# Feed-forward activation turned by VectorE block transposes and SBUF-to-SBUF DMAs instead of TensorE transposes

## The chip, the core and the metric

The kernel runs on one core of one Trainium2 chip. The metric is the device time of one execution in microseconds (us), and lower is better. Engines are named as the profile names them: PE is TensorE (PEld its weight loads), DVE is VectorE, ACT is ScalarE, POOL is GpSimd, SP is SyncE, which here only issues DMAs. A name with a q (ACTq, SPq) is the engine's instruction sequencer.

## What is computed

Two decoder layers over 256 tokens of width 2048, all in float32. Each layer has a mixer and then a SwiGLU feed-forward part; the change lies in the latter alone:

```python
h = rms_norm(x, ffn_norm[l])
gate, up = jnp.split(h @ w_gate_up[l], 2, axis=-1)      # w_gate_up: 2048 x 11264
x = x + ((jax.nn.silu(gate) * up) @ w_down[l]).astype(x.dtype)   # w_down: 5632 x 2048
```

## The kernel before

**Matmuls.** Every large weight is split into a high part `w_hi` and a remainder `w_lo`, and so is every activation, and each product is three matmuls: high by high, high by low, low by high (lines 1475 to 1477). The stationary operand is a 128x128 piece of the turned activation, the moving one 512 columns of the weight. A *slot* is 1 MB of weights, four rows of 128 by 512 columns; it is handled in two *halves*, and PE does 12 matmuls for each half.

**The weight pipeline.** SP loads slot j into one of four places of `raw` (line 338), once VectorE has finished the slot that lay there. ACT rounds a half to `w_hi` (`half_hi`, line 451, after waits for the load and for `half_used`), DVE subtracts it from `raw` to make `w_lo` (`half_lo`, line 890), and PE multiplies. `w_hi` and `w_lo` are rings of four halves, so ACT and DVE write at most four halves ahead of PE: the half (2,0), meaning slot j = 2 and its first half, can be written only when PE has done the half (0,0). In the code `half_used` counts the halves that PE has done.

**The feed-forward part.** The 5632 inner columns are 11 chunks of 512. Each layer does them in two parts, of 6 and of 5 chunk pairs (`PAIRS`). A *pair* is one chunk of gate, slots j = 0 to 3, and the same chunk of up, slots j = 4 to 7. The first pair of a part is written out; the others are a hardware loop on every engine. After its pairs a part multiplies its activation with `w_down`: four output chunks c, each of as many slots as the part has pairs (the *down* phase). There are 22 pairs in all, 18 of them turned inside a loop, 4 of them in a down phase.

**The activation between gate/up and down.** ACT makes `silu` of the gate from PSUM (lines 828, 829) ahead of slot 6. When up is complete, DVE multiplies: two operations write `act_row`, 256 tokens by 512 columns, tokens on partitions (`act_rows`, lines 1402 and 1403). This stands in DVE's program ahead of slot 2 of the next pair, or of slot 2 of the down phase. The down matmul wants columns on partitions, so `act_row` is turned: PE does eight 128x128 transposes into PSUM banks 4 and 5 (`turn`, line 2004), after slot 3 of the next pair, or ahead of slot 3 of the down phase. ACT then copies them to `act_hi` (`turned_hi`, line 840), ahead of slot 6, or after slot 3 in the down phase. DVE writes `act_lo` (`turned_lo`, line 1410). PE waits for `act_lo` ahead of the last slot of output chunk 0.

Each engine runs its own instructions in the order in which the code writes them, and semaphores tie them together. There is no scheduler.

Of the kernel before, what the change touches and what calls it, by code (L numbers as in the profile page):

```python
# [27 lines left out]
F32 = mybir.dt.float32  # L28
# [7 lines left out]
P = 128  # L36
D = 2048
SEQ = 256
TT = SEQ // P
DEPTH = 2  # L40
KT = D // P
CH = 512
# [70 lines left out]
def build(nc, stream, x_in, positions, params, consts, lora, gains, rows, out):  # L113
    with ExitStack() as ctx:
# [49 lines left out]

        gain_row = gain[0:2 * DEPTH * KT, 0:P]
        rstd = small[:, 220:222]
        p_rw = at(RING_END, RW_F, TT, P)
        p_mla = at(RING_END + 3584, TT, 832)
        p_hg = at(RING_END + 5248, TT, 2048)
# [271 lines left out]
        def _(act):  # L441
# [66 lines left out]
            for l in range(DEPTH):  # L508
# [306 lines left out]
                for part, pairs in enumerate(PAIRS):  # L815
                    fresh = part == 0
                    makes_norm = part == len(PAIRS) - 1 and l < DEPTH - 1

                    def pair(i, first):
                        gi, si = i * 2 + g4f, i * 2 + s4f  # L820
                        for j in range(8):
                            if j == 6:

                                act.wait_ge(half_used, chunk_ends(si, 4))
                                if not (first and pair0 == 0):
                                    act.wait_ge(S("act_row_ready"), i + pair0)
                                act.wait_ge(S("rstd_ready"), norm_of_ffn + 1)
                                nc.scalar.activation(silu[:, 0, :], psum[:, 0, :], ACT.Silu, scale=rstd[:, 0:1])
                                nc.scalar.activation(silu[:, 1, :], psum[:, 1, :], ACT.Silu, scale=rstd[:, 1:2]).then_inc(
                                    acc_free[0], 1)  # L830
                                if not first:
                                    turned_hi(i - 1, pair0)
                            split_hi(gi, si, j)
                            if first and fresh:
                                norm_tail(norm_of_ffn, j)

                    def turned_hi(i, p0):
                        act.wait_ge(S("act_turned"), i + (p0 + 1))
                        dst = act_hi[:, bass.ds(i * 4, 4), :] if not isinstance(i, int) else act_hi[:, 4 * i:4 * i + 4, :]
                        nc.scalar.activation(dst, bank(4, 2).rearrange("p (k t) -> p k t", k=4),  # L840
                                             ACT.Copy).then_inc(S("act_hi_ready"), 1)

                    pair(0, True)
                    with act.Fori(1, pairs) as i:
                        pair(i, False)
                    g4f, s4f = g4f + 2 * pairs, s4f + 2 * pairs
                    for j in range(4 * pairs):
                        split_hi(g4f, s4f, j)
                        if j == 3:
                            turned_hi(pairs - 1, pair0)  # L850
                        if makes_norm and j > pairs and j % pairs == 3:
                            x_hi(2 * l + 2, j // pairs - 1)
                            x_squares(2 * l + 2, j // pairs - 1)
                    g4f, s4f = g4f + pairs, s4f + pairs
                    pair0 += pairs
# [3 lines left out]
        def _(dve):  # L859
# [108 lines left out]
            for l in range(DEPTH):  # L968
# [426 lines left out]
                for n, pairs in enumerate(PAIRS):  # L1395
                    def act_rows(i, si, p0):

                        dve.wait_ge(half_used, chunk_ends(si, 8))
                        dve.wait_ge(acc_free[0], i + (gate_base + 2))
                        if not isinstance(i, int) or i + p0 > 0:  # L1400
                            dve.wait_ge(S("act_turned"), i + p0)
                        stt(act_row[:, 0, :], psum[:, 2, :], rstd[:, 0:1], silu[:, 0, :], MUL, MUL)
                        stt(act_row[:, 1, :], psum[:, 3, :], rstd[:, 1:2], silu[:, 1, :], MUL, MUL).then_inc(acc_free[1], 1)
                        dve.wait_ge(acc_free[1], i + (gate_base + 2))
                        dve.sem_inc(S("act_row_ready"), 1)

                    def turned_lo(i, p0):
                        dve.wait_ge(S("act_hi_ready"), i + (p0 + 1))
                        k = bass.ds(i * 4, 4) if not isinstance(i, int) else slice(4 * i, 4 * i + 4)
                        tt(act_lo[:, k, :], bank(4, 2).rearrange("p (k t) -> p k t", k=4), act_hi[:, k, :].bitcast(F32),  # L1410
                           SUB).then_inc(S("act_lo_ready"), 1)

                    gate_base = odd0 + sum(PAIRS[:n]) + 4 * n // 2
# [42 lines left out]
        def _(pe):  # L1456
# [81 lines left out]
            for l in range(DEPTH):  # L1538
# [456 lines left out]
                for part, pairs in enumerate(PAIRS):  # L1995
                    makes_norm = part == len(PAIRS) - 1 and l < DEPTH - 1

                    def turn(i, p0):
                        pe.wait_ge(S("act_row_ready"), i + (p0 + 1))
                        if not isinstance(i, int) or i + p0 > 0:  # L2000
                            pe.wait_ge(S("act_lo_ready"), i + p0)
                        for k in range(4):
                            for t in range(TT):
                                last = tr(bank(4, 2)[:, k * SEQ + t * P:k * SEQ + (t + 1) * P],  # L2004
                                          act_row[:, t, k * P:(k + 1) * P], ident)
                        last.then_inc(S("act_turned"), 1)

                    def pair(i, first):
                        si = i * 2 + s4f
                        for u in range(2):  # L2010
                            pe.wait_ge(acc_free[u], i + (acc + 1))
                            if part == 0 and first and u == 0:
                                for j in range(4):
                                    first_slot(2 * l + 1, si, j, 0)
                            else:
                                slots(si, range(4 * u, 4 * u + 4), 0, KT, 2 * u, hT_hi, hT_lo)
                            if u == 0 and not first:
                                turn(i - 1, pair0)

                    pair(0, True)  # L2020
                    with pe.Fori(1, pairs) as i:
# [2 lines left out]
                    for c in range(4):  # L2024
                        pe.wait_ge(acc_free[c % 2], acc + c // 2 + 1)
                        for j in range(pairs):
                            if c == 0 and j == 3:
                                turn(pairs - 1, pair0)
                            if c == 0 and j == pairs - 1:
                                pe.wait_ge(S("act_lo_ready"), pair0 + pairs)  # L2030
                            if l == DEPTH - 1 and part == len(PAIRS) - 1 and c == 3 and j == pairs - 1:
                                last_slot(s4f, pairs * c + j, 4 * j, 4 * pairs, 2 * (c % 2), act_hi, act_lo)
                                continue
                            slots(s4f, [pairs * c + j], 4 * j, 4 * pairs, 2 * (c % 2), act_hi, act_lo)
                            if makes_norm and c and j == 1:
                                x_turn(2 * l + 2, c - 1)
# [99 lines left out]
```

## Time and profile before

| | us |
|---|---|
| median of 3 runs | 2353.47 |
| range of the runs | 2352.15 to 2355.67 |
| span of the profiled execution | 2351.5 |
| PE busy in it | 2324.1 |
| DVE busy | 1331.0 |
| ACT busy | 1103.5 |

The span goes from the first to the last instruction. Busy times are sums over one engine's instructions. The columns in a view of the timeline are start, duration, engine, line and operation, output and input, and in brackets how long the engine sat idle before it and what ended that. A DMA's own row is the time in which the issuing sequencer was taken; its landing is counted from the issue.

### The profile page before, as it was taken

The page shows a single profiled execution, that of the slowest core. Times are in us where ns is not written, and L with a number is a line of the kernel's source. Part 1 is how long each engine was busy: PE and PEld are TensorE (multiplying, and loading weights), DVE is VectorE, ACT ScalarE, POOL GpSimd, SP SyncE. Part 2 cuts the span into 40 slices and gives each one's busy share as a digit, 9 for nine tenths or more (in the row PEclk, how much of TensorE's full clock was granted, in tenths as well). Part 3 has the DMA queues.
Part 4 walks back from the last instruction along what each step waited for, and adds up shares of the span by engine and source line. Part 5 has one row for each costly group of instructions (what it writes and reads, how often), then busy time and mean ns, then how long its engine had stood idle before and what let it go on. Part 6 is the DMA issues. An engine that isn't in the chain of part 4 may idle for free.

```text
span 2351.5 us, 33396 instructions
## 1 busy us (share of the span) xinstructions
PE 2324.1 (99%) x13481; PEld 1924.8 (82%) x13481; DVE 1331.0 (57%) x1420; ACT 1103.5 (47%) x1362; POOL 55.1 (2%) x58
## 2 busy tenths in 40 slices
PE   8999999999999999999999999999999999999999
PEld 7888688888888888888888886888888888888887
DVE  5686676545445445445557857765454454454454
ACT  6554745544443344444445547454444433444433
POOL 0000110000000000000000002100000000000000
PEclk9999999999999999999999999999999999999999
DMA  7453305555555555554554532044555555555554
GB/s 299 166 184 130 122 21 178 181 195 194 182 195 182 194 196 193 184 194 181 193 184 152 194 115 102 29 171 180 196 189 186 193 184 194 197 191 185 192 184 141
DMA packets 59519, 407.04 MB, mean 173 GB/s; under 512 B 6608, under 2 KB 6704, under 8 KB 13200
## 3 DMA queue, kind: packets, MB, share of 16 engines
q1 hardware_dynamic: 58720, 401.66, 47.9%
q0 software_dynamic: 688, 3.78, 0.5%
q8 instruction: 84, 1.38, 0.2%
q14 instruction: 27, 0.22, 0.0%
HBM read 403.32 MB, written 2.10 MB: 172 GB/s over the span
## 4 chain that ended last, share of the span: by engine, by line
PE 93%; DVE 5%; issue 1%; ACT 0%; DMA 0%; DVEq 0%; SPq 0%; ACTq 0%
PE psum L1475 28%; PE psum L1477 28%; PE psum L1476 28%; PE psum L1669 2%; PE psum L1917 1%; PE psum L2004 1%; PE psum L1764 1%; PE psum L1570 1%; PE psum L1509 1%; DVE arena L1211 1%; DVE arena L1284 0%; DVE arena L1292 0%; DVE small L1194 0%; DVE arena L1188 0%; DVE arena L1178 0%
## 5 line engine op out<-in xcount | busy, mean ns | idle before, releaser
L890 DVE TENSOR_TENSOR w_lo<-raw,w_hi 128x1024 fp32r<-128x1024 f32 (+2 forms) x752 | 901.3, 1205 | 843.9 <-ACT w_hi L451 836.8
L451 ACT ACTIVATE w_hi<-raw 128x1024 fp32r<-128x1024 f32 (+2 forms) x752 | 782.0, 1044 | 1071.8 <-PE psum L1477 1070.2
L1475 PE MATMUL psum<-w_hi,hT_hi 128*128 128x512 f32 (+2 forms) x2128 | 821.6, 386 | 3.1 <-DVE w_lo L890 3.1
L1477 PE MATMUL psum<-w_hi,hT_lo 128*128 128x512 f32 (+2 forms) x2128 | 816.4, 384 | 0.0
L1476 PE MATMUL psum<-w_lo,hT_hi 128*128 128x512 f32 (+2 forms) x2128 | 816.3, 384 | 0.0
L1475 PEld LDWEIGHTS psum<-w_hi,hT_hi 128*128 128x128 f32 x2128 | 399.7, 188 | 81.8 <-DVE w_lo L890 2.4
L1477 PEld LDWEIGHTS psum<-w_hi,hT_lo 128*128 128x128 f32 x2128 | 399.6, 188 | 78.5
L1476 PEld LDWEIGHTS psum<-w_lo,hT_hi 128*128 128x128 f32 x2128 | 399.8, 188 | 76.4
L1475 PE MATMUL psum<-w_hi,act_hi 128*128 128x512 f32 x872 | 340.4, 390 | 0.0
L1477 PE MATMUL psum<-w_hi,act_lo 128*128 128x512 f32 x872 | 339.4, 389 | 0.0
L1476 PE MATMUL psum<-w_lo,act_hi 128*128 128x512 f32 x872 | 339.3, 389 | 0.0
L1477 PEld LDWEIGHTS psum<-w_hi,act_lo 128*128 128x128 f32 x872 | 163.7, 188 | 33.9
L1476 PEld LDWEIGHTS psum<-w_lo,act_hi 128*128 128x128 f32 x872 | 163.7, 188 | 33.7
L1475 PEld LDWEIGHTS psum<-w_hi,act_hi 128*128 128x128 f32 x872 | 163.7, 188 | 33.7
L1669 PE MATMUL psum<-raw,arena 128*128 128x384 f32 (+1 forms) x192 | 72.0, 525 | 0.4
L1669 PEld LDWEIGHTS psum<-raw,arena 128*128 128x128 f32 x192 | 35.3, 190 | 30.9 <-issue 11.8
L1410 DVE TENSOR_TENSOR act_lo<-psum,act_hi 128x1024 f32 (+1 forms) x22 | 26.9, 1224 | 38.6 <-ACT act_hi L840 38.6
L1764 PEld LDWEIGHTS psum<-arena 64*64 64x64 f32 x1024 | 33.3, 142 | 4.0 <-DVE arena L1269 2.2
L1764 PE MATMUL psum<-arena 64*64 64x64 f32 x1024 | 35.3, 227 | 0.6 <-DVE arena L1269 0.6
L902 DVE SCALAR_TENSOR_TENSOR hT_lo<-psum,gain_col,hT_hi 128x256 fp32r<-128x256 f32 x64 | 26.5, 476 | 14.0 <-ACT hT_hi L473 14.0
L840 ACT ACTIVATE act_hi<-psum 128x1024 f32 (+1 forms) x22 | 22.6, 1027 | 20.8 <-PE psum L2004 20.8
L923 DVE TENSOR_TENSOR x<-x,psum 128x1024 f32<-128x1024 f32 x23 | 27.9, 1213 | 4.9 <-PE psum L1477 4.9
(319 smaller groups left out, 1194.7 us busy)
## 6 DMA issues: line engine op xcount, KB each, us to landing
raw<-stream_dram SPq DMA_DIRECT2D x360, 1024.0 KB, 4.8
raw<-stream_dram SPq DMA_DIRECT2D x16, 512.0 KB, 3.7
raw<-stream_dram SPq DMA_DIRECT2D x8, 768.0 KB, 4.3
raw<-stream_dram SPq DMA_DIRECT2D x8, 640.0 KB, 3.8
x<-x_in_dram SPq DMA_DIRECT2D x4, 512.0 KB, 9.2
lor<-lora_dram POOLq DMA_DIRECT2D x2, 832.0 KB, 10.3
con<-consts_dram POOLq DMA_DIRECT2D x1, 1648.0 KB, 11.4
out_dram<-x SPq DMA_DIRECT2D x3, 512.0 KB, 7.3
```

The source lines that it names most:

```text
L451: nc.scalar.activation(w_hi[:, q % HALF_RING, 0:2 * w], raw[:, j % 4, hf * 2 * w:(hf + 1) * 2 * w], ACT.Copy).then_inc(hi_done, 1)
L890: tt(w_lo[:, q % HALF_RING, 0:2 * w], raw[:, j % 4, hf * 2 * w:(hf + 1) * 2 * w], w_hi[:, q % HALF_RING, 0:2 * w].bitcast(F32), SUB).then_ ...
L902: last = stt(hT_lo[:, 4 * c + k, :], bank(x_turn_bank(n, c), 2)[:, k * SEQ:(k + 1) * SEQ], gain_col[:, n * KT + 4 * c + k:n * KT + 4 * c + ...
L923: vs(tt(xs, xs, psum[:, b0:b0 + 2, :], ADD), "x_added", n_added)
L1211: u(ts(z, z, small[:, 64 + off + h:65 + off + h], None, MUL))
L1410: tt(act_lo[:, k, :], bank(4, 2).rearrange("p (k t) -> p k t", k=4), act_hi[:, k, :].bitcast(F32), SUB).then_inc(S("act_lo_ready"), 1)
L1475: mm(o, a_hi, w_hi[:, r, cols], start=(k == 0), stop=False)
L1476: mm(o, a_hi, w_lo[:, r, cols], start=False, stop=False)
L1477: last = mm(o, a_lo, w_hi[:, r, cols], start=False, stop=(k == n_k - 1))
L1509: last = tr(bank(x_turn_bank(n, c), 2)[:, k * SEQ + t * P:k * SEQ + (t + 1) * P], x[:, t, c * CH + k * P:c * CH + (k + 1) * P], ident)
L1669: last = mm(psum[:, UP_BANK[c] + t, 0:w], src[:, k, t * P:(t + 1) * P], raw[:, c % 4, k * w:(k + 1) * w], start=(k == 0), stop=(k == nk - 1))
L1764: last = mm(bank(b0, 2)[hp, m * w:(m + 1) * w], left(hp, n), right(hp, n), start=True, stop=True)
```

## The change

PE no longer turns the activation. `act_row` is written in another layout, one `STREAM_TRANSPOSE` on DVE turns every 32x32 block of it into `act_blocks`, and 16 DMAs from SBUF to SBUF, 32 partitions by 256 elements (32 KB) each, put the blocks on their partitions in `act_moved`. ACT issues these 16 after its slot 2. `turned_hi` and `turned_lo` then read `act_moved` instead of PSUM. The two buffers lie in `gain`, which the feed-forward part doesn't use otherwise.

```diff
+        act_blocks = gain[:, 0:2 * CH]
+        act_moved = gain[:, 2 * CH:4 * CH]
+        n_moves = (P // 32) ** 2
...
                             split_hi(gi, si, j)
+                            if j == 2 and not first:
+                                move_blocks(i - 1, pair0)
...
+                    def move_blocks(i, p0):
+
+                        act.wait_ge(S("act_blocks_turned"), i + (p0 + 1))
+                        if not isinstance(i, int) or i + p0 > 0:
+                            act.wait_ge(S("act_lo_ready"), i + p0)
+                        for q in range(P // 32):
+                            for b in range(P // 32):
+                                act.dma_start(act_moved[32 * q:32 * q + 32, 256 * b:256 * b + 256],
+                                              act_blocks[32 * b:32 * b + 32, 256 * q:256 * q + 256]).then_inc(
+                                                  S("act_moved"), 16)
+
                     def turned_hi(i, p0):
-                        act.wait_ge(S("act_turned"), i + (p0 + 1))
-                        dst = act_hi[:, bass.ds(i * 4, 4), :] if not isinstance(i, int) else act_hi[:, 4 * i:4 * i + 4, :]
-                        nc.scalar.activation(dst, bank(4, 2).rearrange("p (k t) -> p k t", k=4),
+                        act.wait_ge(S("act_moved"), i * (16 * n_moves) + 16 * n_moves * (p0 + 1))
+                        k = bass.ds(i * 4, 4) if not isinstance(i, int) else slice(4 * i, 4 * i + 4)
+                        nc.scalar.activation(act_hi[:, k, :].rearrange("p k (t b e) -> p (k t) b e", t=TT, e=32),
+                                             act_moved.rearrange("p (b n e) -> p n b e", n=8, e=32),
                                              ACT.Copy).then_inc(S("act_hi_ready"), 1)
...
                     for j in range(4 * pairs):
                         split_hi(g4f, s4f, j)
+                        if j == 2:
+                            move_blocks(pairs - 1, pair0)
                         if j == 3:
                             turned_hi(pairs - 1, pair0)
...
-                        stt(act_row[:, 0, :], psum[:, 2, :], rstd[:, 0:1], silu[:, 0, :], MUL, MUL)
-                        stt(act_row[:, 1, :], psum[:, 3, :], rstd[:, 1:2], silu[:, 1, :], MUL, MUL).then_inc(acc_free[1], 1)
+                        for t in range(TT):
+                            last = stt(act_row.rearrange("p a b -> p (a b)").rearrange(
+                                "p (n t r) -> p t n r", n=16, t=TT)[:, t],
+                                psum[:, 2 + t, :].rearrange("p (n r) -> p n r", n=16), rstd[:, t:t + 1],
+                                silu[:, t, :].rearrange("p (n r) -> p n r", n=16), MUL, MUL)
+                        last.then_inc(acc_free[1], 1)
                         dve.wait_ge(acc_free[1], i + (gate_base + 2))
                         dve.sem_inc(S("act_row_ready"), 1)
+                        nc.vector.transpose(act_blocks.rearrange("p (q k n) -> p k q n", q=4, k=4),
+                                            act_row.rearrange("p a b -> p (a b)").rearrange(
+                                                "p (k q n) -> p k q n", k=4, q=4)).then_inc(
+                            S("act_blocks_turned"), 1)
+                        dve.wait_ge(S("act_blocks_turned"), i + (p0 + 1))
...
-                    def turn(i, p0):
-                        pe.wait_ge(S("act_row_ready"), i + (p0 + 1))
-                        if not isinstance(i, int) or i + p0 > 0:
-                            pe.wait_ge(S("act_lo_ready"), i + p0)
-                        for k in range(4):
-                            for t in range(TT):
-                                last = tr(bank(4, 2)[:, k * SEQ + t * P:k * SEQ + (t + 1) * P],
-                                          act_row[:, t, k * P:(k + 1) * P], ident)
-                        last.then_inc(S("act_turned"), 1)
...
-                            if u == 0 and not first:
-                                turn(i - 1, pair0)
...
-                            if c == 0 and j == 3:
-                                turn(pairs - 1, pair0)
```

Line numbers in the listings of the changed program are its own; in them L456 is the old line 451, L911 the old 890, L1504 to L1506 the old 1475 to 1477, and `gain` is where `act_blocks` and `act_moved` lie.

On ACT, inside the loop over pairs, from slot 2 to slot 3. Before:

```order
L450 REGISTER_ALU [waits raw_in2]
L451 ACTIVATE w_hi<-raw 128x1024 [waits half_used]
L450 REGISTER_ALU [waits raw_in2]
L451 ACTIVATE w_hi<-raw 128x1024 [waits half_used]
L450 REGISTER_ALU [waits raw_in3]
L451 ACTIVATE w_hi<-raw 128x1024 [waits half_used]
```

And in the changed program:

```order
L455 REGISTER_ALU [waits raw_in2]
L456 ACTIVATE w_hi<-raw 128x1024 [waits half_used]
L455 REGISTER_ALU [waits raw_in2]
L456 ACTIVATE w_hi<-raw 128x1024 [waits half_used]
L848 REGISTER_ALU [waits act_blocks_turned]
L851 DMA gain<-gain 32x256 [waits act_lo_ready]
L851 DMA gain<-gain 32x256 x15
L455 REGISTER_ALU [waits raw_in3]
L456 ACTIVATE w_hi<-raw 128x1024 [waits half_used]
```

Sixteen DMA issues and a wait for DVE now stand between the half (2,1) and the half (3,0).

On PE, inside the same loop, between slot 3 and slot 4, the last matmul of gate and the first of up. Before:

```order
L1477 MATMUL psum<-w_hi,hT_lo 128x512
L2001 REGISTER_ALU [waits act_row_ready]
L2004 MATMUL psum<-con,act_row 128x128 [waits act_lo_ready]
L2004 MATMUL psum<-con,act_row 128x128 x7
L1467 REGISTER_ALU [waits acc_odd_free]
L1475 MATMUL psum<-w_hi,hT_hi 128x512 [waits w_lo_written]
```

And in the changed program:

```order
L1506 MATMUL psum<-w_hi,hT_lo 128x512
L1496 REGISTER_ALU [waits acc_odd_free]
L1504 MATMUL psum<-w_hi,hT_hi 128x512 [waits w_lo_written]
```

The eight transposes and the two waits ahead of them are gone, and nothing took their place on PE.

On DVE, in the changed program's loop, where the activation is multiplied, just ahead of `w_lo` of the half (2,0):

```order
L1420 REGISTER_ALU [waits half_used]
L1422 SCALAR_TENSOR_TENSOR act_row<-psum,small,silu 128x16x32 [waits acc_even_free]
L1422 SCALAR_TENSOR_TENSOR act_row<-psum,small,silu 128x16x32
L1429 STREAM_TRANSPOSE gain<-act_row 128x4x4x64 [waits acc_odd_free]
L910 REGISTER_ALU [waits act_blocks_turned]
L911 TENSOR_TENSOR w_lo<-raw,w_hi 128x1024 [waits w_hi_written]
```

The block transpose is new; it waits for the two products, and the next half's `w_lo` waits for it.

## Rows read from the trace of the kernel before

**Rows 1.** The page: its head, and the busy time of each engine.

```profile
span 2351.5 us, 33396 instructions
PE 2324.1 (99%) x13481; PEld 1924.8 (82%) x13481; DVE 1331.0 (57%) x1420; ACT 1103.5 (47%) x1362; POOL 55.1 (2%) x58
```

**Rows 2.** Busy time by stretch: stretch, engines, granted clock, DMA share, GB/s.

```profile
423.00:904.00 481.00, 481.00 (x2156) 398.90 (x2154) 239.86 (x211) 204.65 (x213) 0.00 (x0) 1.00 0.54 190
```

**Rows 3.** The page's costliest groups: count, busy and mean ns, idle time before.

```profile
L890 DVE TENSOR_TENSOR w_lo<-raw,w_hi 128x1024 fp32r<-128x1024 f32 (+2 forms) x752 | 901.3, 1205 | 843.9 <-ACT w_hi L451 836.8
L451 ACT ACTIVATE w_hi<-raw 128x1024 fp32r<-128x1024 f32 (+2 forms) x752 | 782.0, 1044 | 1071.8 <-PE psum L1477 1070.2
```

**Rows 4.** Timeline of PE around one turn inside the loop.

```profile
514.36 0.39 PE L1477 MATMUL psum<-w_hi,hT_lo 128*128 128x512 f32 x1
514.59 1.03 PE L2004 MATMUL psum<-con,act_row 128*128 128x128 f32 x8
515.38 0.48 PE L1475 MATMUL psum<-w_hi,hT_hi 128*128 128x512 f32 x1
515.70 0.40 PE L1476 MATMUL psum<-w_lo,hT_hi 128*128 128x512 f32 x1
515.93 0.39 PE L1477 MATMUL psum<-w_hi,hT_lo 128*128 128x512 f32 x1
```

**Rows 5.** All instructions of line 2004: count, ns min/median/max, first and last start.

```profile
L2004 PE MATMUL psum<-con,act_row x176: 270/272/276, 514.6 to 2255.4; 128*128 128x128 f32 x176
```

**Rows 6.** Timeline of DVE over one pair of the loop.

```profile
495.26 0.74 DVE L1402 SCALAR_TENSOR_TENSOR act_row<-psum,small,silu 128x512 f32<-128x512 f32 x1
495.92 0.74 DVE L1403 SCALAR_TENSOR_TENSOR act_row<-psum,small,silu 128x512 f32<-128x512 f32 x1
496.89 1.23 DVE L890 TENSOR_TENSOR w_lo<-raw,w_hi 128x1024 fp32r<-128x1024 f32 x1 [0.22 <-ACT w_hi L451]
...
539.67 0.74 DVE L1402 SCALAR_TENSOR_TENSOR act_row<-psum,small,silu 128x512 f32<-128x512 f32 x1
```

**Rows 7.** Timeline of ACT there: halves (2,0), (2,1) and (3,0).

```profile
495.75 1.06 ACT L451 ACTIVATE w_hi<-raw 128x1024 fp32r<-128x1024 f32 x1 [1.66 <-PE psum L1477]
498.46 1.06 ACT L451 ACTIVATE w_hi<-raw 128x1024 fp32r<-128x1024 f32 x1 [1.66 <-PE psum L1477]
501.19 1.06 ACT L451 ACTIVATE w_hi<-raw 128x1024 fp32r<-128x1024 f32 x1 [1.66 <-PE psum L1477]
```

**Rows 8.** All instructions of line 1284, DVE's block transposes in the mixer.

```profile
L1284 DVE STREAM_TRANSPOSE arena<-arena x18: 711/711/1245, 289.6 to 1499.0; 128x512 f32<-128x512 f32 x16, 128x1024 f32<-128x1024 f32 x2
```

**Rows 9.** Register operations of ACT's sequencer at line 450, from 519 to 524 us.

```profile
L450 ACTq ALU_OP  x2: 35/35/35, 521.1 to 523.8; - x2
```

**Rows 10.** All issues of line 338, in the feed-forward part, and their landing.

```profile
L338 SPq DMA_DIRECT2D raw<-stream_dram x264: 332/333/352, 423.1 to 2318.2; - x132
...
DMA to landing us min/median/max: 4.6/4.8/6.5
```

**Rows 11.** Timeline of SP's first DMA issues, back to back.

```profile
0.75 0.58 SPq L315 DMA_DIRECT2D gain<-gains_dram  x1
1.38 0.57 SPq L313 DMA_DIRECT2D x<-x_in_dram  x1
...
5.51 22.52 SPq L332 DMA_DIRECT2D raw<-stream_dram  x5
```

**Rows 12.** Timeline of POOL: its DMA issues back to back, first and last of six.

```profile
20.85 0.54 POOL L374 DMA_DIRECT2D con<-consts_dram  x1 [18.87 <-DMA raw<-stream_dram]
...
23.50 0.54 POOL L383 DMA_DIRECT2D lor<-lora_dram  x1
```

**Rows 13.** Landing of line 315's one DMA, 32 KB.

```profile
DMA to landing us min/median/max: 2.0/2.0/2.0
```

**Rows 14.** Timeline of ACT in a down phase: halves (2,0), (3,1), `act_hi`, (4,0).

```profile
717.92 1.06 ACT L451 ACTIVATE w_hi<-raw 128x1024 fp32r<-128x1024 f32 x1 [1.66 <-PE psum L1477]
...
726.09 1.06 ACT L451 ACTIVATE w_hi<-raw 128x1024 fp32r<-128x1024 f32 x1 [1.66 <-PE psum L1477]
732.35 1.03 ACT L840 ACTIVATE act_hi<-psum 128x1024 fp32r<-128x1024 f32 x1 [5.20 <-PE psum L2004]
733.27 2.96 ACT L451 ACTIVATE w_hi<-raw 128x1024 fp32r<-128x1024 f32 x3
```

More of the change, by code:

```diff
@@ L1399, in act_rows @@
                         dve.wait_ge(acc_free[0], i + (gate_base + 2))
-                        if not isinstance(i, int) or i + p0 > 0:
-                            dve.wait_ge(S("act_turned"), i + p0)
-                        stt(act_row[:, 0, :], psum[:, 2, :], rstd[:, 0:1], silu[:, 0, :], MUL, MUL)
-                        stt(act_row[:, 1, :], psum[:, 3, :], rstd[:, 1:2], silu[:, 1, :], MUL, MUL).then_inc(acc_free[1], 1)
+                        for t in range(TT):
[4 more added lines that the diff above has]
+                        last.then_inc(acc_free[1], 1)
                         dve.wait_ge(acc_free[1], i + (gate_base + 2))
                         dve.sem_inc(S("act_row_ready"), 1)
+                        nc.vector.transpose(act_blocks.rearrange("p (q k n) -> p k q n", q=4, k=4),
[3 more added lines that the diff above has]
+                        dve.wait_ge(S("act_blocks_turned"), i + (p0 + 1))
                     def turned_lo(i, p0):
@@ L1409, in turned_lo @@
                         k = bass.ds(i * 4, 4) if not isinstance(i, int) else slice(4 * i, 4 * i + 4)
-                        tt(act_lo[:, k, :], bank(4, 2).rearrange("p (k t) -> p k t", k=4), act_hi[:, k, :].bitcast(F32),
+                        hi, lo = (z[:, k, :].rearrange("p k (t b e) -> p (k t) b e", t=TT, e=32) for z in (act_hi, act_lo))
+                        tt(lo, act_moved.rearrange("p (b n e) -> p n b e", n=8, e=32), hi.bitcast(F32),
                            SUB).then_inc(S("act_lo_ready"), 1)
@@ L1996, in _ @@
                     makes_norm = part == len(PAIRS) - 1 and l < DEPTH - 1
-                    def turn(i, p0):
-                        pe.wait_ge(S("act_row_ready"), i + (p0 + 1))
-                        if not isinstance(i, int) or i + p0 > 0:
-                            pe.wait_ge(S("act_lo_ready"), i + p0)
-                        for k in range(4):
-                            for t in range(TT):
-                                last = tr(bank(4, 2)[:, k * SEQ + t * P:k * SEQ + (t + 1) * P],
-                                          act_row[:, t, k * P:(k + 1) * P], ident)
-                        last.then_inc(S("act_turned"), 1)
                     def pair(i, first):
```

## The prediction, made before the change was run

> **What bounds the kernel now.** I read the page first, then the busy time by stretch, then the timeline of one pair. The page has PE busy for 2324.1 of 2351.5 us and the next engine, DVE, for 1331.0 [rows 1]. In a stretch wholly inside the feed-forward part PE is busy for 481.00 of 481.00 us, at a granted clock of 1.00, its 2.4 GHz level, while DVE and ACT are busy for half or less of it [rows 2]. The costliest groups say who waits for whom: ACT's `w_hi` was idle 1071.8 us, nearly all until PE had used a half, and DVE's `w_lo` 843.9 us until ACT had written one [rows 3]. So in this part PE sets the pace and the other two stand ready four halves ahead. Whatever leaves PE shortens the kernel by its full time, as long as no weight half comes late. Whatever is added to ACT or DVE is free until it has eaten that lead.
>
> **What is removed: 22 turns on PE.** In the timeline, neighbouring matmuls start 0.227 us apart. Without the turn the matmul after the one at 514.36 would start at 514.59, and the two behind it at 514.81 and 515.04. They start at 515.38, 515.70 and 515.93 [rows 4], and from there on the old step is back. So one turn takes 515.93 - 515.04 = 0.89 us from PE, less than the 1.03 us of its row, since its ends overlap with the neighbours. The same comes out another way: from one pair's product to the next is 539.67 - 495.26 = 44.41 us [rows 6], and 16 halves of 2.72 us (501.19 - 495.75 over two, [rows 7]) are 43.52. There are 176 transposes, eight to a turn, so 22 turns [rows 5], and 22 x 0.89 = 19.5 us.
>
> Rows 4 and 5 put one 128x128 transpose at 0.11 us of PE's time. The Trainium skill (VectorE: DVE Perf Modes, The three transpose paths) gives a bf16 one on TensorE as 390 ns; an estimate by that page would make the removal worth 22 x 8 x 0.39 = 69 us. The measured gaps decide against that. The same page's Rules for kernel authors advise TensorE for a 128x128 transpose if PSUM will do as its destination, which speaks against this change.
>
> **What is added on DVE.** The two products keep their size and count, so they stay at 0.74 us each [rows 6]; their output is in runs of 32 elements, and I take no extra for that. The block transpose of 128x1024 took 1245 ns in the mixer, and 711 ns for half of it [rows 8]. The new one has four dimensions; I take 1.25 us, and even twice that would be hidden: `w_lo` of the half (2,0) now starts at about 496.9 + 1.25 = 498.1 instead of 496.89, and ends at 499.4. I put PE's first matmul of this pair at 514.59 - 8 x 2.72 = 492.83, so it needs (2,0) at 492.83 + 4 x 2.72 = 503.7. Nothing is late.
>
> **What is added on ACT: 16 DMA issues, and this decides.** They stand between the halves (2,1) and (3,0). Queued behind them are (3,0) on ACT, `w_lo` of (3,0) on DVE, and PE. The time they may take, in the clock of [rows 7]:
> - Start. The blocks are turned at about 498.2. ACT's sequencer gets past the half (2,1) when that starts, at 498.46. Register operations ran at 521.1 and 523.8 [rows 9], one for each half's start and not all at once, so the sequencer does not pass a waiting instruction, but it need not wait for a running one to end. So the issues start at about 498.55; if a DMA must wait for the running operation to end, at 498.46 + 1.06 = 499.52.
> - End. PE needs (3,0) at 492.83 + 6 x 2.72 = 509.15. From `w_hi`'s start to `w_lo`'s end is (496.89 + 1.23) - 495.75 = 2.37 us [rows 6, 7]. So ACT must be free by 506.78.
>
> This leaves 8.23 us, or 0.51 us for each issue, with the earlier start, and 7.26 us, or 0.45 us, with the later. No row shows an issue on ACT. The nearest, from below: SP's issues of 1 MB in this same part took 0.333 us each, alone [rows 10]; with a gap of 0.05 us between two (1.38 - 0.75 - 0.58, [rows 11]) that is 0.38 us, and 16 are 6.1 us. From above: SP's first eight issues, back to back, came every (5.51 - 0.75) / 8 = 0.595 us [rows 11], and 16 are 9.5 us. In between lies POOL, which generates its own descriptors: (23.50 - 20.85) / 5 = 0.53 us [rows 12], 8.5 us. I take 0.38 us. The 264 issues of [rows 10] are in the same stage and within 20 ns of each other, while the slow ones of [rows 11] stand at the cold start and move far larger pieces, of mixed tensors. Then ACT is free at 504.6 (505.6 with the later start), 2.1 (1.2) us ahead of need, and catches up at once, because a half takes it 1.06 us and PE 2.72. That it can catch up is on record: in a down phase ACT stood still until 732.35 for the turned activation and then wrote three halves in 2.96 us [rows 14], with PE never idle in that stretch [rows 2]. The cost at 0.38 us is nothing. Beyond 0.51 (0.45) us each further 0.1 us costs 1.6 us in each of the 22 turns.
>
> **The transfers.** 16 DMAs of 32 KB are 0.5 MB in a pair whose weights are 8 MB. A 32 KB load landed 2.0 us after issue [rows 13], so the last block lands at about 506.6; by the slowest weight load, 6.5 us [rows 10], at 511. Inside the loop ACT asks for them ahead of slot 6, whose half (6,0) stands 6 x 2.72 us behind (3,0)'s 501.19, at about 517, which is late enough for both. In a down phase it asks after (3,1). There the old wait lasted until 732.35, which is 14.43 us after (2,0) at 717.92 [rows 14], or 510.2 in the clock used above. Landing at 506.6 is 3.6 us earlier than the old turn; landing at 511 is 0.9 us later, four times in the kernel, at most 4 us. For the weight loads the DMA share is 0.54 [rows 2] and they land in 4.8 us; a place in `raw` is freed some 16.7 us ahead of its use (7 halves of 2.72 less the 2.37 us of chain), so they stay hidden.
>
> The Trainium skill (DMA: Bandwidth & Descriptors, Measured) says that transfers under 64 KB are dominated by their descriptors. By it these copies move slowly; since their landing has slack, the sum stays as it is.
>
> `turned_hi` and `turned_lo` read SBUF instead of PSUM. ACT and DVE already do this shape from SBUF in 1.06 and 1.23 us [rows 6, 7], so I count nothing.
>
> **The sum.** Span 2351.5 - 19.5 = 2332.0 us. The median of the runs is 2.0 us above this span, so **2334.0 us** against 2353.5, or 0.83% less.
>
> **Rival 1: ACT's issues become PE's wait, and the kernel is slower.** Place: the half (3,0) of each of 22 turns. It costs more than it brings when 16 issues exceed 8.23 + 0.89 = 9.12 us, 0.57 us each (with the later start 8.15 us, 0.51 us). At the 0.595 us of [rows 11] the wait is 9.52 - 8.23 = 1.29 us, the net +0.40 a turn, 2362; with the later start 2.26 us, +1.37 a turn, 2384. For it: those eight rows are the only back-to-back ones on a sequencer of this kind, and sixteen at once is what the change does. Against it: [rows 10]. An issue of 1 us would give some 2500 and I leave it beyond the range. Chance 0.27. It is also how the rule for TensorE, cited above, would come true.
>
> **Rival 2: issues of about 0.53 us eat most of the gain.** At POOL's pace [rows 12] the wait is 0.25 us, and the result 2353.5 - 22 x 0.64 = 2339; with the later start the wait is 1.22 us and the result 2361. So one price ends on either side. What ends within 0.2% of before needs a wait of 0.68 to 1.10 us a turn, a narrow band. Chance 0.09.
>
> **Rival 3: the turned activation comes late in the down phases.** By the bounds above at most about 4 us, so 2338, still faster. Chance 0.04.
>
> **Rival 4: the change doesn't do what it says.** The transposes do leave PE, but another wait could stand in the same place: the accumulator banks of up, which DVE frees with the second product at 496.66, 18 us before PE wants them. That leaves no room for it. Chance 0.01.
>
> **How the numbers follow.** The forecast, no new wait on PE, has 0.59. Rival 2 has 0.09, of which 0.03 lie on the faster side and 0.06 within 0.2%. With rival 3 (0.04, faster) and rival 4 (0.01, within) faster by over 0.2% has 0.66, within 0.2% 0.07, and slower by over 0.2% 0.27, rival 1's. 0.2%, 4.7 us, is about what a measurement of this kernel can tell from no change. The range runs from 2331, since nothing but the turns leaves PE and 3 us covers the reading of the 0.89, to 2375, which takes in rival 2 and the lower half of rival 1; the upper half stays out with about 0.13, and what lies under 2331 with 0.03. The likeliest case's own range is 2331 to 2340.
>
> **What would show each step right or wrong.** The turns: line 2004 gone and PE's starts 0.227 us apart from gate to up. The cover: PE's row of waits for `w_lo` stays at a few us in all; if rival 1 holds, it shows PE idle 22 times ahead of the half (3,0), released by `w_lo`. The price: the duration and the spacing of ACTq's DMA issues, 0.38 us forecast, 0.51 where it begins to cost, and whether the first starts beside the half (2,1) or behind it. DVE: a block transpose of about 1.25 us, 22 times. The landing: ACT's wait for the moved blocks, none in the loop, and in the down phases shorter than the 5.2 us that the old one took [rows 14]. The forecast fails if an issue on ACT takes over 0.5 us, if the weight loads land so late that ACT waits for `raw`, or if the granted clock falls below 1.00.

## Result and profile after

| | before | changed |
|---|---|---|
| median of the runs, us | 2354.57 | 2419.98 |
| range of the runs, us | 2352.15 to 2355.80 | 2416.43 to 2424.21 |
| span of the profiled execution, us | 2351.5 | 2414.9 |
| mean granted PE clock | 0.999 | 0.986 |

The ratio is 1.0279, with a 95% interval of 1.0264 to 1.0294: 2.8% slower, where 0.8% faster was forecast. The time lies beyond the range's end at 2375.

The page of the changed kernel, its head, engines, the chain that ended last, and the groups that answer to [rows 1, 3]:

```profile
span 2414.9 us, 33409 instructions
PE 2339.1 (97%) x13305; PEld 1925.2 (80%) x13305; DVE 1351.7 (56%) x1442; ACT 1095.2 (45%) x1362; POOL 55.0 (2%) x58
...
PE 81%; ACTq 9%; DVE 6%; ACT 1%; issue 1%; DMA 0%; SPq 0%; DVEq 0%
...
L456 ACT ACTIVATE w_hi<-raw 128x1024 fp32r<-128x1024 f32 (+2 forms) x752 | 775.7, 1043 | 1166.4 <-PE psum L1506 983.8
L1504 PE MATMUL psum<-w_hi,hT_hi 128*128 128x512 f32 (+2 forms) x2128 | 831.8, 391 | 41.4 <-DVE w_lo L911 41.4
...
L1504 PE MATMUL psum<-w_hi,act_hi 128*128 128x512 f32 x872 | 342.8, 393 | 10.8 <-DVE w_lo L911 10.8
```

The transposes are gone: 13305 matmuls instead of 13481, 176 fewer. But PE now stood idle 52.2 us (41.4 + 10.8) for `w_lo`, and ACT's sequencer, which had no share in the chain before, holds 9% of it. In the feed-forward part there are 22 waits, one ahead of each half (3,0). All three links of one such wait stand in the timelines of ACT, DVE and PE. ACT, from the half (2,0) of the second loop pair on:

```profile
543.42 1.07 ACT L456 ACTIVATE w_hi<-raw 128x1024 fp32r<-128x1024 f32 x1 [1.66 <-PE psum L1506]
546.14 1.06 ACT L456 ACTIVATE w_hi<-raw 128x1024 fp32r<-128x1024 f32 x1 [1.65 <-PE psum L1506]
546.22 10.29 ACTq L851 DMA_DIRECT2D gain<-gain  x16
556.63 3.90 ACT L456 ACTIVATE w_hi<-raw 128x1024 fp32r<-128x1024 f32 x4 [9.43 <-issue]
```

DVE over the same pair:

```profile
542.93 1.40 DVE L1422 SCALAR_TENSOR_TENSOR act_row<-psum,small,silu 128x512 f32<-128x512 f32 x2
544.49 1.25 DVE L1429 STREAM_TRANSPOSE gain<-act_row 128x1024 f32<-128x1024 f32 x1
545.86 1.23 DVE L911 TENSOR_TENSOR w_lo<-raw,w_hi 128x1024 fp32r<-128x1024 f32 x1
547.24 1.23 DVE L911 TENSOR_TENSOR w_lo<-raw,w_hi 128x1024 fp32r<-128x1024 f32 x1 [0.15 <-ACT w_hi L456]
557.72 4.63 DVE L911 TENSOR_TENSOR w_lo<-raw,w_hi 128x1024 fp32r<-128x1024 f32 x4 [9.26 <-ACT w_hi L456]
```

PE, at the half (3,0):

```profile
556.37 0.39 PE L1505 MATMUL psum<-w_lo,hT_hi 128*128 128x512 f32 x1
556.59 0.39 PE L1506 MATMUL psum<-w_hi,hT_lo 128*128 128x512 f32 x1
559.00 0.70 PE L1504 MATMUL psum<-w_hi,hT_hi 128*128 128x512 f32 x1 [2.02 <-DVE w_lo L911]
559.50 0.63 PE L1505 MATMUL psum<-w_lo,hT_hi 128*128 128x512 f32 x1
559.92 0.63 PE L1506 MATMUL psum<-w_hi,hT_lo 128*128 128x512 f32 x1
...
562.06 0.62 PE L1505 MATMUL psum<-w_lo,hT_hi 128*128 128x512 f32 x1
562.48 0.43 PE L1506 MATMUL psum<-w_hi,hT_lo 128*128 128x512 f32 x1
562.75 0.39 PE L1504 MATMUL psum<-w_hi,hT_hi 128*128 128x512 f32 x1
562.98 0.40 PE L1505 MATMUL psum<-w_lo,hT_hi 128*128 128x512 f32 x1
```

Sixteen issues keep ACT's sequencer for 10.3 us, `w_hi` of (3,0) starts at 556.63, its `w_lo` at 557.72, and PE, which was ready at about 556.8, starts at 559.00: 559.00 - 556.59 - 0.227 = 2.18 us late. Then something that the prediction had no price for: the next matmuls start 0.43 us apart instead of 0.227. The busy time by stretch (columns as in [rows 2]: PE, PEld, DVE, ACT, POOL, then the granted clock, DMA share and GB/s):

```profile
555.00:559.00 4.00, 1.98 (x10) 1.32 (x8) 1.28 (x2) 2.37 (x3) 0.00 (x0) 1.00 0.13 33
559.00:563.00 4.00, 4.00 (x11) 3.14 (x12) 3.35 (x3) 1.52 (x2) 0.00 (x0) 0.57 0.40 117
563.00:567.00 4.00, 4.00 (x19) 3.31 (x18) 1.23 (x1) 1.68 (x2) 0.00 (x0) 1.00 1.00 406
```

After 2 us of idleness the granted clock was 0.57 over 4 us, mostly the 1.2 GHz level, and then 1.00 again, the 2.4 GHz level. From 559.00 to 562.98 PE takes ten steps in 3.98 us where 2.27 were due, 1.71 us lost.

**The sum for this pair**: -0.89 (turn) + 2.18 (wait) + 1.71 (clock) = +3.0 us. For the whole kernel: 22 x -0.89 = -19.5; idle for `w_lo` 52.2 less the 3.1 of before [PE's row for line 1475 on the page of before], plus 0.16 us for each of 22 waits that the idle figure leaves out (2.18 against 2.02), +52.6; and behind 17 of the 22 waits PE's matmuls step at 0.43 us for a while, 17 x 1.71 = +29. Together +62; the spans differ by 63.4. (Added up one by one in the trace, the 17 come to 31 us: fifteen lost 1.5 to 1.8 us, two lost 2.6 and 3.0.)

The pair shown stands for most, but not for all. In 18 of the 22 turns the sixteen issues took 10.2 to 10.4 us and PE stood idle 1.9 to 2.2 us. In the first turn and in the last, a down phase's, of each layer they took 11.2 to 12.0 us, because single issues among them read up to 1.88 us, and PE stood idle 3.0 to 3.8 us. Why those issues are long is not shown.

### The profile page after: what moved, and what is told of

The parts are those of the page before. It is cut to its first block, busy times and chain, and to the rows that moved or that the text cites. A ratio compares the mean times of both kernels' runs of the same rounds, so it can differ in the third digit from the quotient of the medians.

```text
span 2414.9 us, 33409 instructions
## 1 busy us (share of the span) xinstructions
PE 2339.1 (97%) x13305; PEld 1925.2 (80%) x13305; DVE 1351.7 (56%) x1442; ACT 1095.2 (45%) x1362; POOL 55.0 (2%) x58
## 4 chain that ended last, share of the span: by engine, by line
PE 81%; ACTq 9%; DVE 6%; ACT 1%; issue 1%; DMA 0%; SPq 0%; DVEq 0%
PE psum L1504 25%; PE psum L1505 25%; PE psum L1506 25%; ACTq L851 9%; PE psum L1698 2%; DVE w_lo L911 1%; PE psum L1946 1%; ACT w_hi L456 1%; PE psum L1793 1%; PE psum L1599 1%; PE psum L1538 1%; DVE arena L1232 1%; DVE arena L1305 0%; DVE arena L1313 0%; DMA x<-x_in_dram 0%
## 5 line engine op out<-in xcount | busy, mean ns | idle before, releaser
L911 DVE TENSOR_TENSOR w_lo<-raw,w_hi 128x1024 fp32r<-128x1024 f32 (+2 forms) x752 | 896.2, 1204 | 905.8 <-ACT w_hi L456 895.5
L456 ACT ACTIVATE w_hi<-raw 128x1024 fp32r<-128x1024 f32 (+2 forms) x752 | 775.7, 1043 | 1166.4 <-PE psum L1506 983.8
L1504 PE MATMUL psum<-w_hi,hT_hi 128*128 128x512 f32 (+2 forms) x2128 | 831.8, 391 | 41.4 <-DVE w_lo L911 41.4
L1505 PE MATMUL psum<-w_lo,hT_hi 128*128 128x512 f32 (+2 forms) x2128 | 825.8, 388 | 0.0
L1506 PE MATMUL psum<-w_hi,hT_lo 128*128 128x512 f32 (+2 forms) x2128 | 825.4, 388 | 0.0
L1504 PEld LDWEIGHTS psum<-w_hi,hT_hi 128*128 128x128 f32 x2128 | 405.4, 190 | 129.8 <-DVE w_lo L911 48.6
L1506 PEld LDWEIGHTS psum<-w_hi,hT_lo 128*128 128x128 f32 x2128 | 405.3, 190 | 80.8
L1505 PEld LDWEIGHTS psum<-w_lo,hT_hi 128*128 128x128 f32 x2128 | 405.4, 191 | 78.7
L1504 PE MATMUL psum<-w_hi,act_hi 128*128 128x512 f32 x872 | 342.8, 393 | 10.8 <-DVE w_lo L911 10.8
L1506 PE MATMUL psum<-w_hi,act_lo 128*128 128x512 f32 x872 | 341.3, 391 | 0.0
L1504 PEld LDWEIGHTS psum<-w_hi,act_hi 128*128 128x128 f32 x872 | 165.0, 189 | 46.7 <-DVE w_lo L911 12.5
L1506 PEld LDWEIGHTS psum<-w_hi,act_lo 128*128 128x128 f32 x872 | 164.9, 189 | 34.6
L1439 DVE TENSOR_TENSOR act_lo<-gain,act_hi 128x1024 f32 (+1 forms) x22 | 26.9, 1224 | 18.4 <-ACT act_hi L858 18.4
L1422 DVE SCALAR_TENSOR_TENSOR act_row<-psum,small,silu 128x512 f32<-128x512 f32 x44 | 30.9, 743 | 0.0
## 6 DMA issues: line engine op xcount, KB each, us to landing
lor<-lora_dram POOLq DMA_DIRECT2D x2, 832.0 KB, 10.8
```

What stands on the lines that cost most here:

```text
L456: nc.scalar.activation(w_hi[:, q % HALF_RING, 0:2 * w], raw[:, j % 4, hf * 2 * w:(hf + 1) * 2 * w], ACT.Copy).then_inc(hi_done, 1)
L911: tt(w_lo[:, q % HALF_RING, 0:2 * w], raw[:, j % 4, hf * 2 * w:(hf + 1) * 2 * w], w_hi[:, q % HALF_RING, 0:2 * w].bitcast(F32), SUB).then_ ...
L1422: last = stt(act_row.rearrange("p a b -> p (a b)").rearrange("p (n t r) -> p t n r", n=16, t=TT)[:, t], psum[:, 2 + t, :].rearrange("p (n ...
L1439: tt(lo, act_moved.rearrange("p (b n e) -> p n b e", n=8, e=32), hi.bitcast(F32), SUB).then_inc(S("act_lo_ready"), 1)
L1504: mm(o, a_hi, w_hi[:, r, cols], start=(k == 0), stop=False)
L1505: mm(o, a_hi, w_lo[:, r, cols], start=False, stop=False)
```

## Experiments

**Theory A**: the issues hold ACT's sequencer longer than its lead over PE, PE waits for that, and the clock falls because PE waits. **Rival B**: DVE's longer block or the new reads from SBUF hold the pipeline. **Rival C**: the copies' traffic does. **Rival D**: the clock falls for another reason. Each experiment was timed beside the kernel before anew: it took 2352.1 us beside the first four, 2352.6 beside the next four, and 2353.6 in one run beside the last four. And one question inside theory A: why does an issue cost 0.61 us when SP's loads cost 0.333 [rows 10]?

### The change without its copies

```diff
-                        for q in range(P // 32):
-                            for b in range(P // 32):
-                                act.dma_start(act_moved[...], act_blocks[...]).then_inc(S("act_moved"), 16)
...
-                                             act_moved.rearrange("p (b n e) -> p n b e", n=8, e=32),
+                                             act_blocks.rearrange("p (b n e) -> p n b e", n=8, e=32),
```

> The changed kernel without its 16 copies: act_hi is read from the unmoved blocks, so the activation that goes into the down product is not the reference's. Everything else of the change stays: the new layout of act_row, DVE's block transpose, act_hi and act_lo from SBUF. Theory A (the time in which ACT issues the copies is what PE waits for, and the clock falls after the wait): no wait at all, the full gain of the turns, 2334 us. Rival B (DVE's longer block, or the new reads from SBUF, hold the pipeline): PE still waits for w_lo, 2380 us or more.

Measured: 2332.1 us, ratio 0.9913 (0.9897 to 0.9930). PE never waits in the feed-forward part; what it is idle for `w_lo` elsewhere, 3.1 us, is the 3.1 us of the kernel before. So DVE's block transpose, the new layouts and the reads from SBUF cost nothing: rival B falls. This is also the whole gain that the removal of the turns can give, 2352.1 - 2332.1 = 20.0 us against the forecast 19.5.

### The kernel before, with the issues added

```diff
                             split_hi(gi, si, j)
+                            if j == 2 and not first:
+                                move_blocks(i - 1, pair0)
...
                     def turned_hi(i, p0):
+                        act.wait_ge(S("act_moved"), i * (16 * n_moves) + 16 * n_moves * (p0 + 1))
                         act.wait_ge(S("act_turned"), i + (p0 + 1))
```

> The kernel before, with its TensorE turns, plus the 16 copies a pair on ACT at the changed kernel's place; nothing reads what they copy, ACT only waits for them ahead of act_hi. Theory A: ACT is taken for 10.3 us, PE waits 2.0 us idle in each of 22 pairs and the clock falls after most of them, so 2354 + 22 x (2.2 + 1.3) + the rest = 2430 to 2440 us. Rival B: without the block transpose the wait disappears, 2354 us.

Measured: 2421.6 us, ratio 1.0300 (1.0282 to 1.0317). The sixteen copies alone, with TensorE's turns kept and DVE untouched, bring the loss. It is a little under what was expected: only 10 of the 22 waits were followed by matmuls at 0.43 us, against 17 in the changed kernel, and the four waits in the down phases lasted 1.1 us only. What decides whether a wait of 2 us costs the clock isn't shown.

### The same issues, spread over ACT's halves

```diff
+LOOP_MOVES = {5: (0, 4), 6: (4, 7), 7: (7, 10), 8: (10, 12), 9: (12, 14), 10: (14, 16)}
+DOWN_MOVES = {5: (0, 6), 6: (6, 11), 7: (11, 16)}
...
+                            for hf in range(2):
+                                half_hi(gi, si, j, hf)
+                                if not first and 2 * j + hf in LOOP_MOVES:
+                                    move_blocks(i - 1, pair0, *LOOP_MOVES[2 * j + hf])
```

> The changed kernel with the same 16 issues on ACT, but 4, 3, 3, 2, 2, 2 of them behind six successive halves of the loop, from (2,1) on, and 6, 5, 5 behind three halves in a down phase, where act_hi and act_lo then come behind the first half of slot 4. Theory A: no half is late by more than the lead, 2334 us, or up to 2345 if the down phases lose some. Rival C (the copies' traffic, or the sequencer time in total, is what costs): as the changed kernel, about 2420 us. It also shows the price of an issue that follows a pause.

Measured: 2336.8 us, ratio 0.9930 (0.9913 to 0.9946). Same 352 copies, same engine, and PE waits for no `w_lo` in the feed-forward part: rival C falls, and ACT's total sequencer time is no problem, only its length in one piece. Two new waits stand in its down phases:

```profile
PE psum L1510 <- DVE act_lo L1444: 3.9, 2, 2.4
```

There `act_hi` comes later than in the changed kernel, behind the first half of slot 4, and it waited for the copies to land. That wait, with one fall of the clock behind it (1.5 us), is about what this kernel is slower than the kernel without copies. ACT's timeline, one pair:

```profile
542.14 1.06 ACT L458 ACTIVATE w_hi<-raw 128x1024 fp32r<-128x1024 f32 x1 [1.66 <-PE psum L1512]
542.22 2.56 ACTq L855 DMA_DIRECT2D gain<-gain  x4
545.00 1.06 ACT L458 ACTIVATE w_hi<-raw 128x1024 fp32r<-128x1024 f32 x1 [1.80 <-PE psum L1512]
545.02 1.80 ACTq L855 DMA_DIRECT2D gain<-gain  x3
...
553.02 1.06 ACT L458 ACTIVATE w_hi<-raw 128x1024 fp32r<-128x1024 f32 x1 [1.66 <-PE psum L1512]
553.03 1.26 ACTq L855 DMA_DIRECT2D gain<-gain  x2
```

Each group starts as soon as the half ahead of it has started and runs beside it.

### The issues on SP

```diff
+                    for i in range(1, pairs):
+                        for j in range(8):
+                            ffn_load(i, at_slot, j)
+                            if j == 5:
+                                move_blocks(i - 1, pair0)
```

(`move_blocks` is the same, with `sp` for `act`; `ffn_load` is SP's load with constants in place of the loop's registers.)

> The changed kernel with the 16 issues on SP, behind its load of slot 5, and SP's loop in the feed-forward part written out so that its waits are constants. SP has some 12 us of lead on the loads. Theory A: 2334 us. It also settles the price of an issue: if 0.61 us is ACT's own price, SP's rows for the same copies read 0.33 us; if it is the price of copies in close succession or of SBUF to SBUF, they read 0.6 us as on ACT. Rival C (traffic): about 2420 us.

Measured: 2331.8 us, ratio 0.9911 (0.9895 to 0.9928). This kernel makes every copy, and it is faster than both kernels. PE never waits in the feed-forward part. SP's rows for the copies and one timeline of it:

```profile
L354 SPq DMA_DIRECT2D gain<-gain x352: 507/591/1724, 498.3 to 2234.0; - x176
...
DMA to landing us min/median/max: 1.8/1.8/3.2
```

```profile
539.12 0.33 SPq L346 DMA_DIRECT2D raw<-stream_dram  x1
541.84 10.02 SPq L354 DMA_DIRECT2D gain<-gain  x16
551.91 3.86 SPq L346 DMA_DIRECT2D raw<-stream_dram  x3
```

A load takes SP 0.33 us, and the sixteen copies after it 10.02 us. So 0.6 us is the price of these copies on either sequencer and not ACT's. SP can afford it: three loads go out only behind the copies, and PE is never late for it.

### Twelve and fourteen issues

```diff
-        n_moves = (P // 32) ** 2
+        n_moves = 12
...
+                        for n in range(n_moves):
+                            q, b = n // 4, n % 4
```

> The changed kernel with only 12 of its 16 copies (the last four block rows aren't moved, so act_hi holds stale values there). Theory A: 12 x 0.645 = 7.7 us is inside the 8.2 us of lead, no wait of PE, 2332 to 2336 us. Rival C (each copy costs by its traffic): three quarters of the loss, about 2398 us.

> The changed kernel with only 14 of its 16 copies (the last two aren't made, act_hi holds stale values there). Theory A: 14 x 0.645 = 9.0 us, 0.8 us over the lead in 22 pairs, so 2332 + 22 x 1.0 = 2354 us if the clock stays at 1.00 after so short a wait, and about 2380 if it falls as after the 2 us waits.

Measured: with twelve 2335.6 us (ratio 0.9931, 0.9914 to 0.9947), PE idle twice in the feed-forward part, for 0.46 and 0.14 us; with fourteen 2365.6 us (1.0044, 1.0030 to 1.0059). (The twelve leave the median 3.5 us above the kernel without copies; the trace accounts for about 1 us of it, and the rest isn't explained.) So the step lies between 7.9 us of issues (one group of twelve is a row of 7.88 us) and 9.0, where the prediction had put the lead, 8.2 us. The loss doesn't grow with the copies but sets in there, which rival C can't give. With fourteen PE was idle 24.2 us in its 22 waits, 18 of them 0.65 to 1.5 us long, and only two, of 1.8 and 2.1 us, were followed by matmuls at the lower clock; two of 2.2 and 2.4 us were not. 2332 + 24.2 + 22 x 0.16 + 2 x 1.7 = 2363. The 2354 that I expected had 0.8 us a wait; they averaged 1.1.

### The wait filled with work

```diff
                     for hf in range(2):
                         q = 2 * j + hf
+                        if fill == q:
+                            keep_busy(18)
```

> The changed kernel with 18 transposes of the identity on PE into an unused bank ahead of the half (3,0), 18 x 0.11 = 2.0 us of work in the place of the wait; the output is the reference's. Theory A (the clock falls because PE stands idle there): the granted clock stays at 1.00, matmuls behind keep their 0.227 us, and the time is 2420 less about 30, 2390 us. Rival D (the clock falls for another reason): no change, or slower than 2420.

Measured: 2386.6 us, ratio 1.0151 (1.0134 to 1.0167), granted clock 0.999 on the mean. PE's timeline at a half (3,0):

```profile
556.15 0.39 PE L1508 MATMUL psum<-w_hi,hT_lo 128*128 128x512 f32 x1
556.38 2.12 PE L1547 MATMUL psum<-con 128*128 128x128 f32 x18
558.66 0.50 PE L1506 MATMUL psum<-w_hi,hT_hi 128*128 128x512 f32 x1 [0.15 <-DVE w_lo L911]
559.00 0.40 PE L1507 MATMUL psum<-w_lo,hT_hi 128*128 128x512 f32 x1
559.23 0.39 PE L1508 MATMUL psum<-w_hi,hT_lo 128*128 128x512 f32 x1
```

The half (3,0) is as late as ever, but the steps behind it are 0.23 us. Useless work in the place of the idle time gives back 2420.0 - 2386.6 = 33.4 us: that is the clock's part of the loss, shown apart from the wait's, which is the rest of the way to the kernel without copies, 2386.6 - 2332.1 = 54.5 us. The fall of the clock hangs on PE standing idle there: rival D falls.

### The issues on GpSimd

```diff
+                for n in range(sum(PAIRS) * l, sum(PAIRS) * (l + 1)):
+                    pool.wait_ge(S("act_blocks_turned"), n + 1)
...
+                            pool.dma_start(act_moved[...], act_blocks[...]).then_inc(S("act_moved"), 16)
```

> The changed kernel with the 16 issues on GpSimd, which has nothing else to do in the feed-forward part and nothing queued behind them. At the 0.53 us of its rows 16 take 8.5 us. Theory A: 2332 us, as with SP. If VectorE's work or the descriptors hold GpSimd up, the copies land late and the down phases lose some us: 2335 to 2345.

Measured: 2332.8 us, ratio 0.9914 (0.9897 to 0.9930), PE never waits in the feed-forward part. Sixteen issues take GpSimd 7.8 to 7.9 us in nearly every turn, 0.498 us each, and nothing stands behind them.

### What an issue costs

Four kernels of one run each, all with the issues on ACT at the changed kernel's place. None of them puts the whole activation in its places. The edit is only the form of the transfer, given here in short:

```diff
+ 8 KB:          act_moved[32q:32q+32, 256b:256b+64]  <- act_blocks[32b:32b+32, 256q:256q+64]      x16
+ 128 partitions: act_moved[:, 64n:64n+64]            <- act_blocks[:, 64n:64n+64]                x16
+ from HBM:      act_moved[32q:32q+32, 256b:256b+256] <- stream[4q+b, 32b:32b+32, 256q:256q+256]   x16
+ four copies:   act_moved[:, 256n:256n+256]          <- act_blocks[:, 256n:256n+256]             x4
```

> The changed kernel with 16 copies of 32x64 elements, 8 KB instead of 32 KB each, a quarter of the activation moved. If the issue's 0.61 us hangs on the bytes, it falls towards 0.4 us and PE's wait goes (2335 us); if it hangs on the number of rows or on both sides lying in SBUF, it stays 0.61 us and the time about 2415 us. I expect the second.

> The changed kernel with 16 copies of 128 partitions by 64 elements, 32 KB each, partitions kept, so the blocks aren't put in their places. Same bytes, four times the rows. If the number of rows sets the issue, it goes above 0.61 us and the time above 2420; if 32 partitions are what makes it slow, it falls towards SP's 0.33 us and the time to 2335.

> The changed kernel with its 16 transfers of 32x256 elements read from the weight stream in HBM instead of from the blocks in SBUF, so that act_hi holds no activation. If it is the two SBUF sides that make an issue cost 0.51 to 0.61 us where SP's loads cost 0.33, the rows read about 0.33 to 0.43 us and PE's wait goes (2335 us); if it is something that all 32-partition transfers share, 0.61 us and 2415 us.

> The changed kernel with 4 copies of 128 partitions by 256 elements, 128 KB each, partitions kept, so the blocks aren't put in their places: the same 0.5 MB a pair in a quarter of the issues. Theory A: 4 issues take about 2.5 us, no wait of PE, 2332 us. Rival C (bytes moved): about 2415 us.

Measured: 2421.8, 2437.7, 2339.8 and 2331.0 us. All issues by the trace: number, ns min/median/max, first and last start; in this order, the changed kernel's own row first.

```profile
L851 ACTq DMA_DIRECT2D gain<-gain x352: 514/612/1882, 498.0 to 2314.5; - x176
```

```profile
L851 ACTq DMA_DIRECT2D gain<-gain x352: 514/612/1813, 500.0 to 2319.3; - x176
```

```profile
L850 ACTq DMA_DIRECT2D gain<-gain x352: 472/622/1696, 498.7 to 2334.0; - x176
```

```profile
L851 ACTq DMA_DIRECT2D gain<-stream_dram x352: 317/443/1558, 498.8 to 2239.1; - x176
```

```profile
L850 ACTq DMA_DIRECT2D gain<-gain x88: 472/622/1599, 498.7 to 2224.9; - x88
```

A quarter of the bytes changes nothing. The source does: from HBM the median falls from 0.612 to 0.443 us. And succession does: in the changed kernel the first issue of a turn reads 0.519 us at the median over the 22 turns, and in the spread kernel the first of each group mostly 0.51 to 0.53, while most of those behind it read 0.61; in the HBM form the first reads 0.320 and most of those behind it 0.443. The first issue from HBM thus costs about 0.32 us on ACT, near SP's 0.33 for a lone load [rows 10]; following another costs 0.09 to 0.12 more, and a source in SBUF 0.17 to 0.20 more.

With 128 partitions most issues read 0.622 us, but the second of a turn reads 0.96 at the median (0.66 in the changed kernel). So sixteen take 10.6 us or more where the changed kernel's take 10.2 or more. This form is 17.7 us over the changed kernel: its 22 waits come to 61 us of idleness against 49, and behind 21 of them the clock fell, against 17. Why the second issue is long isn't shown. The four large copies carry the same 0.5 MB a pair in 2.7 to 2.8 us of issues, and leave the full gain, again against rival C.

## Why the prediction was wrong

- **PE sets the pace, and the turns cost 0.89 us each.** Right: without copies the kernel gains 20.0 us, forecast 19.5.
- **DVE's block transpose**, forecast 1.25 us and hidden. Right: 1.25 us, 22 times, no effect.
- **The lead, 8.23 us, and the start beside the running half.** Right, and to a few tenths: the first issue starts 0.08 to 0.15 us behind the start of the half (2,1), and 12 issues go all but unnoticed while 14 don't.
- **The price of an issue, 0.38 us. This is the step that failed.** It was 0.64 us with the gap, 10.3 us for sixteen (11.2 to 12.0 in four turns). Put into the prediction's own formula, 10.3 - 8.23 = 2.1 us of wait, which is what PE shows. The prediction had 0.595 us as its upper end, from the only issues in a row on such a sequencer that the trace of before held [rows 11], and set it aside because they came at a cold start with large pieces. [rows 10] won for its 264 consistent issues, but those were lone ones from HBM: neither of the two conditions that the change brings, one right behind another, and both sides in SBUF. The size was no reason to set [rows 11] aside: their first issue is line 315's of 32 KB [rows 13] and took 0.58 us, while those of [rows 10] move 1 MB at 0.333 us. The issue above 0.5 us and the clock below 1.00, which the prediction named as signs of its failing, both came. The bound should have been open above as well, since no row had an SBUF source.
- **Rival 1 was the case that came**, with the right place (the half (3,0), 22 times) and released by `w_lo`. It was priced at +0.40 to +1.37 us a turn; it came to +3.0 in the pair shown and to 63.4 / 22 = +2.9 on the mean. Of what the +0.40 lacked on the mean, 1.1 us is the longer wait, 2.40 us in place of 1.29, and 1.4 us the clock; in the pair shown it is 0.9 and 1.7 us. So even this rival, at its dearest 2384 us, fell 36 us short of the 2420.
- **The clock** stood in the prediction as a condition at the very end, without a price. [rows 2] show 1.00, but a stretch in which PE never idles can't show what idling costs. It was 33 us, half of the distance to the kernel before.
- **The transfers.** Right that they hide: landing took a median of 2.2 us, where the one 32 KB load of before took 2.0 [rows 13], and the loads kept their 4.8.
- **Rival 2's price**, 0.53 us from GpSimd's rows, was near what GpSimd took for these copies, 0.498 us; moved there, the issues cost nothing.

**A price for the clock stood in the trace of before**, outside the feed-forward part: six transposes in a row at full clock, the same six behind a wait of 2.89 us, and the busy time of the stretch around the latter (columns as above).

```profile
314.75 0.87 PE L1737 MATMUL psum<-con,arena 128*128 128x128 f32 x6
324.31 1.54 PE L1737 MATMUL psum<-con,arena 128*128 128x128 f32 x6 [2.89 <-DVEq L1213]
```

```profile
324.00:327.00 3.00, 2.69 (x28) 2.36 (x30) 1.43 (x2) 0.81 (x1) 0.00 (x0) 0.50 0.00 0
```

Behind the wait the granted clock was 0.50, the 1.2 GHz level, and the same six took 1.54 us in place of 0.87. Rival 1, which ends in a wait of 1.29 to 2.26 us on PE, could have been given a bound for the clock from these rows.

## What to carry to other kernels

Count DMA issues as instructions of the engine that issues them: n in a row on a compute engine are one long instruction, to be set against that engine's lead over its consumer in one piece, so either spread them or give them to a sequencer behind which nothing urgent is queued. Take an issue's price from rows of the same kind, with the same memories on both sides and the same succession, and where none exists keep the range open upward. When a rival ends in a wait of the busiest engine, price the clock too: here a wait of 2.2 us mostly cost 1.7 us more after it had ended.

## Of the hardware, not expected

- The first issue of a row from SBUF to SBUF held ACT's sequencer 0.51 us and those behind it 0.61; from HBM it was 0.32 and 0.44. SP's copies read 0.51 and 0.59, with a lone load from HBM at 0.33. It was the same with 8 KB as with 32 KB. With 128 partitions, at 32 KB as at 128 KB, it was 0.47 and 0.62, but 0.96 for the second.
- The granted clock fell at or after waits of about 2 us, behind 17 of 22 in one kernel and 10 of 22 in another, and after none of the waits of up to 1.5 us in the kernel with fourteen issues. It fell with the first matmul behind the wait in some turns and several matmuls later in others. Transposes of the identity in the gap kept it at 1.00.
- A DMA issue doesn't wait for the ACTIVATE ahead of it on ACT: it started 0.08 to 0.15 us behind its start and ran beside it.
